# Rounded high and low parts for the heads' projections and three gate tiles; gathered rows in quarter rows turned by VectorE

## The reference

```python
h = modulate(rmsnorm(x, norm_mix), shift1, scale1)
proj = h @ w_in                      # q, k, v, o (4 heads x 256 each), gates, u, ga, gb
q, k, v, o, gates, u, ga, gb = split(proj, IN_SPLITS)
# mLSTM: per head chunkwise scan of q, k, v with gates from the columns `gates`, times sigmoid(o)
# S5: complex-diagonal scan of u, gelu(z) * sigmoid(z @ w_glu + b_glu)
merged = sigmoid(ga) * (h_a @ w_pA) + sigmoid(gb) * (h_b @ w_pB)
x = x + gate1 * (merged @ w_out)
h = modulate(rmsnorm(x, norm_ffn), shift2, scale2)
# expert choice: each of 16 experts takes its top 64 latent and top 16 context tokens
aff = softmax(h @ w_router + b_router); topv, topi = top_k(aff.T, cap)
xe = h[topi]
hid = silu(xe @ w1) * (xe @ w3)      # 1024 -> 1536
x = x + gate2 * scatter_add((hid @ w2) * topv)
y = rmsnorm(x, norm_final)
```

## Time and profile before

| what | value |
|---|---|
| median of 3 runs | 1770.94 us (1770.35 to 1771.46) |
| the profiled execution | 1768.68 us, span 1766.9 us |
| mean granted TensorE clock | 0.971 |
| TensorE (matmul) busy | 1646.3 us, 93% |
| VectorE busy | 602.6 us, 34% |
| ACT busy | 355.5 us, 20% |
| POOL busy | 61.1 us, 3% |
| moved by DMA | 418.68 MB, mean 237 GB/s |

### The profile page before, as it was taken

The page is one execution under the profiler, slowest core; times in us unless marked ns, Lnnn a source line. Parts: engine busy times, 40 slices in busy tenths (PEclk is TensorE's granted clock), DMA queues, the critical chain, the costliest instruction groups (busy, mean ns, idle before and its releaser), DMA issues. The chain is left out here.

```text
span 1766.9 us, 33347 instructions
## 1 busy us (share of the span) xinstructions
PE 1646.3 (93%) x15118; PEld 934.8 (53%) x15118; DVE 602.6 (34%) x1351; ACT 355.5 (20%) x731; POOL 61.1 (3%) x76
## 2 busy tenths in 40 slices
PE   5999999999999999798975999999999999999992
PEld 2566665546464564598963344444444444444441
DVE  6878961013112131477645011111111111111113
ACT  5243332122212223355333000000000000000001
POOL 0000000000000000000001000000000000000000
PEclk9999999999999999999998999999999999999996
DMA  9345463101102021143307899999999999999974
GB/s 391 121 145 178 154 224 141 48 0 70 50 0 107 12 84 56 41 173 125 144 36 302 317 401 397 407 407 406 408 409 407 407 407 408 414 411 410 417 310 134
DMA packets 56913, 418.68 MB, mean 237 GB/s; under 512 B 10932, under 2 KB 17716, under 8 KB 27076
## 3 DMA queue, kind: packets, MB, share of 16 engines
q1 hardware_dynamic: 49188, 385.09, 54.6%
q0 software_dynamic: 6864, 28.85, 5.3%
q10 hardware_dynamic: 720, 2.62, 0.4%
HBM read 389.98 MB, written 24.42 MB: 235 GB/s over the span
## 5 line engine op out<-in xcount | busy, mean ns | idle before, releaser
L1780 PE MATMUL bank<-place,x 128*32 128x384 f32 x3120 | 258.1, 489 | 0.9 <-ACT x L1831 0.9
L1780 PE MATMUL bank<-ring_tail,x 128*32 128x384 f32 x3024 | 248.2, 486 | 0.0
L1780 PEld LDWEIGHTS bank<-place,x 128*32 128x32 f32 x3120 | 100.4, 110 | 147.3 <-issue 143.9
L1780 PEld LDWEIGHTS bank<-ring_tail,x 128*32 128x32 f32 x3024 | 97.8, 110 | 142.9 <-issue 141.6
L1870 DVE TENSOR_TENSOR xT<-sq,bank 128x384 f32<-128x384 f32 x48 | 23.7, 549 | 435.8 <-issue 362.3
L1856 DVE SCALAR_TENSOR_TENSOR hT<-bank,gvr,xT 32x256 f32<-32x256 f32 (+1 forms) x192 | 92.1, 480 | 201.0 <-PE bank L1802 198.4
L1099 PE MATMUL bank<-place,hT 128*128 128x512 f32 x320 | 138.0, 592 | 0.0
L244 PE MATMUL bank<-hT,xT 128*128 128x512 f32 x256 | 131.9, 597 | 1.1 <-ACT qk L254 0.9
L1802 PE MATMUL bank<-place,xT 128*32 128x256 f32 x2304 | 126.7, 379 | 0.0
L1802 PE MATMUL bank<-ring_tail,xT 128*32 128x256 f32 x2304 | 126.5, 379 | 0.0
L1831 ACT ACTIVATE x<-bank 128x320 f32<-128x320 f32 x32 | 12.2, 434 | 542.1 <-PE bank L1765 542.1
(11 more groups left out here) (353 smaller groups left out, 1827.8 us busy)
## 6 DMA issues: line engine op xcount, KB each, us to landing
place<-w_e_dram SPq DMA_DIRECT2D x97, 1536.0 KB, 17.8
ring_tail<-w_e_dram SPq DMA_DIRECT2D x95, 1536.0 KB, 17.2
place<-w_ada_dram SPq DMA_DIRECT2D x12, 2048.0 KB, 9.9
xT<-w_gate_dram POOLq DMA_DIRECT2D x8, 1024.0 KB, 6.4
place<-w_qk_dram SPq DMA_DIRECT2D x4, 2048.0 KB, 11.3
place<-w_vo_dram SPq DMA_DIRECT2D x4, 2048.0 KB, 10.8
place<-w_pAB_dram SPq DMA_DIRECT2D x4, 1536.0 KB, 7.7
hT<-gates_dram SPq DMA_DIRECT2D x4, 1280.0 KB, 5.9
```

What stands on the lines that cost most here:

```text
L1780: mm = pe.matmul(PS[bank + j][TJ * g:TJ * g + TJ, 0:FC], x[:, e % 2, 2 * c + k, TJ * j:TJ * j + TJ], w[:, k, FC * g:FC * g + FC], start=(c ...
```

## The change

Three parts.

**Projections.** `hT` is split once into `h_high` (fp32r, in the region of `xT`, by ACT) and `h_low` (in place of `hT`, by VectorE). The weights of a head are taken in four chunks of 256 columns (`chunk_end`, `chunk_of`); each chunk is rounded by ACT (`round_weights`) into one of two buffers in what was the third slot of the ring, and its remainder is written over the raw weights by VectorE (`split_weights`). `project_features` (q, k and gate tiles) and `project_tokens` (v and o) make three products each, into three banks instead of two. The gate tiles 13 to 15 come as one more piece, `w_gtail`, in two chunks. The GLU comes ahead of the first projection instead of between its units. The ring has two slots for the heads, and the slots and the order of loads for the merge block change.

**Gather.** The routing block also computes, per expert and quarter row, an index 4 x token + quarter (`topq`, `gidx4`). `gather` becomes three indirect DMAs of 128 quarter rows (1 KB) each. VectorE turns them with one transpose of 32 x 32 blocks (`turn_x`), and the rows of w_e1 and w_e3 are put in that order by the host. TensorE's transposes, ACT's `take_x` and POOL's memset go.

**Queues.** SP, ACT, VectorE and TensorE take these steps in the order of the diff, cut to its core:

```diff
+        NU = 16
+        NU_S5 = 13
+        NCH = 4 * H + 2
+        UNITS = 18
+        def chunk_end(c):
+            return UNITS * (c // 4) + ((4, 8, 13, 18)[c % 4] if c < 4 * H else (4, 6)[c - 4 * H])
+        for h in range(H):
+            plan.append((ar["w_qk"][h], "units_done", chunk_end(4 * h + 1), 0))
+            plan.append((ar["w_vo"][h], "units_done", chunk_end(4 * h + 3), 1))
+        plan.append((ar["w_gtail"], "units_done", chunk_end(NCH - 1), 0))
+        def chunk_of(memory, c):
+            if c < 4 * H:
+                x, n, at = memory[:, 2 * (c % 4 // 2):2 * (c % 4 // 2) + 2], 512, 256 * (c % 2)
+            else:
+                x, n, at = memory[:, 0:2], 384, 256 * (c % 2)
+            return x.rearrange("p x n -> p (x n)")[:, 0:KD * n].rearrange("p (k n) -> p k n", k=KD)[:, :, at:min(at + 256, n)]
+        def chunk_raw(c):
+            return chunk_of(place, c)
+        def chunk_low(c):
+            return chunk_of(place_r, c)
+        def chunk_high(c):
+            n = 256 if c + 1 < NCH else P
+            return place_r[:, 4 + c % 2, 0:KD * n].rearrange("p (k n) -> p k n", k=KD)
...
+        MERGE_SLOTS = (1, 2, 0, 2, 0, 1)
...
-                load_weights(sp, CH_H + NSLOT)
+                load_weights(sp, CH_H + 2)
                 for h in range(H):
                     if h:
+                        load_weights(sp, CH_H + 2 * h + 3)
...
+                def project_features(c, u):
+                    pe.wait_ge(sem("w_low_ready"), c + 1)
+                    high, low = chunk_high(c), chunk_low(c)
+                    for m in range(high.shape[2] // P):
+                        for x in range(2):
+                            bank_free(u)
+                            t = slice(x * TH, (x + 1) * TH)
+                            n = slice(m * P, (m + 1) * P)
+                            for k in range(KD):
+                                pe.matmul(PS[u % 3][:, 0:TH], high[:, k, n], h_high[:, k, t], start=(k == 0), stop=False)
+                                pe.matmul(PS[u % 3][:, 0:TH], high[:, k, n], h_low[:, k, t], start=False, stop=False)
+                                mm = pe.matmul(PS[u % 3][:, 0:TH], low[:, k, n], h_high[:, k, t], start=False,
+                                               stop=(k == 7))
+                            mm.then_inc(sem("units_done"), 1)
+                            u += 1
+                def project_tokens(c, u):
+                    pe.wait_ge(sem("w_low_ready"), c + 1)
+                    high, low = chunk_high(c), chunk_low(c)
+                    for t in range(NT):
+                        bank_free(u)
+                        tt = slice(t * P, (t + 1) * P)
+                        for k in range(KD):
+                            pe.matmul(PS[u % 3][:, 0:DH], h_high[:, k, tt], high[:, k, :], start=(k == 0), stop=False)
+                            pe.matmul(PS[u % 3][:, 0:DH], h_high[:, k, tt], low[:, k, :], start=False, stop=False)
+                            mm = pe.matmul(PS[u % 3][:, 0:DH], h_low[:, k, tt], high[:, k, :], start=False,
+                                           stop=(k == 7))
+                        mm.then_inc(sem("units_done"), 1)
+                        u += 1
                 def proj_qk(h):
...
+                for m in range(4):
+                    glu(m)
+                pe.wait_ge(sem("h_low_ready"), KD)
                 proj_qk(0)
...
+                def round_weights(c):
+                    if c < NCH:
+                        have_weights(act, chunk_piece(c))
+                        if c >= 2:
+                            act.wait_ge(sem("units_done"), chunk_end(c - 2))
+                        act.activation(chunk_high(c), chunk_raw(c), ACT.Copy).then_inc(sem("w_high_ready"), 1)
...
+                    for j in range(8):
+                        m, t = j // 2, slice(j % 2 * TH, (j % 2 + 1) * TH)
+                        u = UNITS * h + j
+                        act.wait_ge(sem("units_done"), u + 1)
+                        act.activation(qk[:, h % 2, m, t], PS[u % 3][:, 0:TH], ACT.Copy,
                                        scale=DH ** -0.5 if m < 2 else 1.0).then_inc(sem("proj_copied"), 1)
-                    act.wait_ge(sem("qk_done"), 5 * h + 5)
-                    for x in range(2):
-                        ins = act.activation(qk[:, h % 2, 2 * x:2 * x + 2, LAT:TOK],
-                                             PS[2][:, 256 * x:256 * x + 256].rearrange("p (m t) -> p m t", m=2),
-                                             ACT.Copy, scale=1.0 if x else DH ** -0.5)
-                    ins.then_inc(sem("proj_copied"), 1)
+                        if j % 4 == 0:
+                            round_weights(4 * h + j // 4 + 1)
...
+                    for j in range(2 * NT):
+                        u = UNITS * h + 8 + j
+                        act.wait_ge(sem("units_done"), u + 1)
+                        if j < NT:
+                            act.activation(vt[:, h % 2, j, 0:DH], PS[u % 3][:, 0:DH],
+                                           ACT.Copy).then_inc(sem("proj_copied"), 1)
+                        else:
+                            act.activation(og[:, h % 2, j - NT, :], PS[u % 3][:, 0:DH],
+                                           ACT.Sigmoid).then_inc(sem("proj_copied"), 1)
+                        if j % NT == 0:
+                            round_weights(4 * h + j // NT + 3)
...
+                act.wait_ge(sem("gate_out0"), 16 * 7)
+                act.wait_ge(sem("gate_out1"), 16 * 6)
+                for k in range(KD):
+                    act.activation(h_high[:, k, :], hT[:, k, :], ACT.Copy).then_inc(sem("h_high_ready"), 1)
+                round_weights(0)
                 act.wait_ge(sem("z_in"), 8)
                 for m in range(4):
                     act.activation(hbT[:, m, :], zT[:, m, :], ACT.Gelu_apprx_tanh).then_inc(sem("gelu"), 1)
+                for m in range(4):
+                    glu_sigmoid(m)
...
+                def split_weights(c):
+                    dve.wait_ge(sem("w_high_ready"), c + 1)
+                    dve.tensor_tensor(chunk_low(c), chunk_raw(c), chunk_high(c).bitcast(F32),
+                                      ALU.subtract).then_inc(sem("w_low_ready"), 1)
...
+                    if h + 1 < H:
+                        split_weights(4 * h + 7)
+                        split_weights(4 * h + 8)
...
+                for k in range(KD):
+                    dve.wait_ge(sem("h_high_ready"), k + 1)
+                    dve.tensor_tensor(h_low[:, k, :], hT[:, k, :], h_high[:, k, :].bitcast(F32),
+                                      ALU.subtract).then_inc(sem("h_low_ready"), 1)
+                split_weights(0)
...
+                for c in range(1, 5):
+                    split_weights(c)
                 for h in range(H):
                     weigh(h)
+                    for c in range(4 * h + 5, min(4 * h + 7, NCH)):
+                        split_weights(c)
                     combine(h)
...
-                    load_weights(sp, CH_M + m + 2)
                     sp.wait_ge(sem("branch_used"), 8 * (m - 1))
                     load_sigmoids(m)
+                    load_weights(sp, CH_M + m + 2)
...
+                v(dve.tensor_scalar(topf[:, CAPL:CAP], topf[:, CAPL:CAP], float(LAT), None, ALU.add))
+                for j in range(NJ):
+                    n = min(TJ, CAP - TJ * j)
+                    for g in range(NG):
+                        ins = dve.tensor_scalar(topq[:, j, g, 0:n], topf[:, TJ * j:TJ * j + n], 4.0, float(g),
+                                                ALU.mult, ALU.add)
+                ins.then_inc(sem("route_step"), 1)
...
-                    pool.indirect_dma_start(out=xe[:, e % 2, :], out_offset=None, in_=ar["h2"][:, :],
-                                            in_offset=bass.IndirectOffsetOnAxis(ap=gidx[:, e:e + 1], axis=0)
-                                            ).then_inc(sem(f"xe_in{e % 2}"), 16)
+                    for j in range(NJ):
+                        pool.indirect_dma_start(out=xe[:, e % 2, j, :], out_offset=None, in_=h2q,
+                                                in_offset=bass.IndirectOffsetOnAxis(ap=gidx4[:, j, e:e + 1], axis=0)
+                                                ).then_inc(sem(f"xe_in{e % 2}"), 16)
...
-                        if name == "w1" and c == 1 and e + 1 < E:
-                            turn_x(e + 1)
...
+                def turn_x(e):
+                    dve.wait_ge(sem(f"xe_in{e % 2}"), 16 * NJ * (e // 2 + 1))
+                    if e >= 2:
+                        dve.wait_ge(sem("piece_used"), piece_at["w3", e - 2, 3] + 1)
+                    dve.transpose(x[:, e % 2].rearrange("p j k c -> p (j k c)"),
+                                  xe[:, e % 2].rearrange("p j d -> p (j d)")).then_inc(sem("x_turned"), 1)
+                turn_x(0)
                 dve.wait_ge(sem("gate2_ready"), 1)
                 for e in range(E):
```

(2 more changed lines are left out.)

## The result

The changed kernel takes 1712.65 us (median of 4 runs, 1711.69 to 1713.13) where the kernel before takes 1771.2 (4 runs beside it, 1770.35 to 1772.22): a ratio of 0.967, 95% interval 0.965 to 0.969, 58.5 us less. The forecast was 1717, with 1704 to 1740 as its range. The profiled execution took 1712.79 us, with a span of 1710.9 against 1766.9: 56.0 less. (The profiled execution before lay 2.5 us under its median, so the pair of traces shows that much less than the runs.)

What follows compares the result with a forecast made beforehand. The prediction took TensorE to bound the heads, with DMA as busy as TensorE in the expert stage. Its terms, -47.7 + 1.7 - 7.0 + 4.2 - 5.0 = -53.8 us, gave 1714.9 profiled and a median of 1717, range 1704 to 1740.

Steps and rivals of the forecast that it cites:

- The projections: Head projections on TensorE: 57.0 us per head in place of 68.9, -47.7 us over four heads.
- Rival (c): Head projections: a 256-column product costs as much as one of 320, +26 us, 1743; chance 6%.
- (e): Head projections: weight loads are not hidden behind one-pass products, +256 us, near 2027; chance 2%.
- Preparation at nothing: Rounding and splitting of weight chunks on ACT and VectorE: ready at 8.9 us, over five us spare, costed at nothing.
- Rival (d): Weight chunks in the heads: preparation comes late, 1.5 us at each of 16 chunks, +24 us, 1741; chance 5%.
- Gate tiles: Two gate-tile stretches of 18.5 and 9.7 us become 144 products, 21.2 us: -7.0 us.
- Start of the block: GLU moved ahead of the first projection must wait for VectorE's copies of the turned blocks: +1.7 us, bounds 0 and +6.
- Routing and first gather: From top-k to first expert: extra routing operations +2.4, first gather as three indirect DMAs +1.8, together +4.2 us.
- Expert stage: TensorE loses the turns (12.0 us), but gathers 0.4 us dearer let DMA set the pace late: -5.0 us.
- Rival (a): Expert stage: TensorE keeps the pace, -12.0 us in place of -5.0, 1710; chance 14%.
- Rival (b): Expert stage: gathers cost the lagging DMA engines 1.5 us more each, +14 us, 1731; chance 12%.
- the queue change in the merge stage is costed at nothing: Merge-stage weight loads: the changed queue leaves every piece at least eight steps (14 us), so no cost.

Runs made afterwards that it cites:

- prep_2: Changed kernel with ACT rounding and VectorE going over each weight chunk twice, from the second chunk on; 1710.14 us, ratio 0.966 to the kernel before.
- prep_3: Changed kernel with ACT rounding and VectorE going over each weight chunk three times, from the second chunk on; 1750.13 us, ratio 0.988 to the kernel before.

## Why the prediction was right, point by point

**The projections** (-47.7 forecast, -48.7 measured) were right by their mechanism and to 1 us: TensorE sets the time, 0.147 us holds for 320 columns, and 0.120, worked out for 256, is 0.119. Rival (c) is refuted by it, and so is (e), whose 2027 left out the -6 of the other terms (2021). The windows above have TensorE's loads busy as long as its products, 0.188 us each under products of 0.119: they are hidden, all rows in use. By the rule cited from the Trainium skill (TensorE: Matmul & The Clock Gate, The mechanism) they would not be; here the trace disagrees, as the earlier trace rows had said.

**Preparation at nothing**: right. Ready 8.4 us into the chunk (8.9 forecast), and the two runs with more passes show both the cover and its end. Rival (d) is refuted.

**Gate tiles** (-7.0): exact. **Start of the block** (+1.7 forecast, +2.9 measured): the wait for VectorE is there and comes to 2.1 us (5.8 us from the turning of z to the GLU, for 3.7 to the first projection). The other 0.8 is the clock, which the forecast left out: it is at half from 279 to 289, and costs the GLU 2.2 us where it cost the first projection 1.4 before.

**Routing and first gather** (+4.2 forecast, -0.1 measured): two parts, of which the second failed. The routing costs about what was said, +2.4 (twelve operations 1.08 us, another memset; from the same step of the top-k to the first issue 13.1 us for 11.1, +2.0). The gather was mis-sized, +1.8 forecast and -2.2 measured: the three issues of 1.0 us and the gaps of 0.3 came as forecast, but VectorE has the rows 3.1 us behind the end of the third issue, where TensorE had them 6.8 us behind the end of the one, and one VectorE transpose of 0.98 us stands in the place of TensorE, ACT and their handovers.

**Expert stage** (-5.0 forecast, -12.4 measured): the step that failed is the price of the gather, "I take +0.4, near the 1 KB row", with "The lower end is 0". Measured it is -0.6 us per expert. The forecast priced the gather's own packets alone and put what they do to the weights beside them at nothing, without a reason. For the packets themselves it was wrong in form and near in size: they move as 96 packets of 4 KB and not as 384 of 1 KB, and cost +0.1 us. But the weights beside the old gather were slowed, 535 to 539 ns per packet for 469, and the new gather took that away. (304 more packets per expert would be 4864 more on q0. There are 624: 256 of 4 KB and 496 of 4 bytes more, and 128 fewer of one load of gate weights. That load and the larger gathers are 1 MB each, so that q0 moves 28.85 MB before and after by chance.) The weights' DMA needed 734.0 us from the first expert to the last landing (743.9 before), and TensorE 746.0. Rival (a) is what happened: 46.50 us to the end, landings of 26.7 us. "So what looks like 12.0 us is mostly taken back" is wrong: it is kept whole. Rival (b) is refuted. The best guess on the rings that GpSimd's DMAs keep (the Trainium skill, DMA: Bandwidth & Descriptors, Latency and other measured facts) would have made more indirect DMAs dearer on the late engines; no run shows such a price.

**What the forecast left out** took back what the last two terms gave, so that the total still came out near 1717. The drain behind the new gather costs +2.6 (the end has +2.3 in all); it takes 5.27 us in the traces of seven kernels with that gather, the change among them, and 2.65 in the three with the old one. The barrier behind the heads costs +3.2: "the queue change in the merge stage is costed at nothing" asked only whether the weights are late, not what they run beside. And the scores at a lower clock cost +3.1. That is no accident of one execution: in ten of the twelve traces with the changed heads the scores of the second and of the third head take 13.0 us, and in the two with the old heads 11.43 to 11.47 (`prep_2` has 10.28 at one of the places, `prep_3` 11.38 at both). Over the heads' block the granted clock is at half for 20.5 us in both traces with the old heads, and for 30.7 to 34.1 us in nine of those with the new. The five terms of the sum came to -65.2 in place of -53.8, and what had stood at nothing to +9.2 (the 1.7 us ahead of the block are among them).

So the time lies near the forecast for a mixed reason, in part by luck: the heads came by their mechanism, routing and experts brought 11.7 us more than forecast, the experts by rival (a), and three small costs that were left out took most of it back.

**Open**: why the drain takes 2.6 us more (it took 5.06 with twice as many gathers, so it does not go by their number), what lowers the granted clock behind a turn and more so with the changed heads, and which property of the old gather slows the weights beside it.

## What to carry to other kernels

Price a product by its columns and passes from the trace, and then ask of every DMA that a change moves which barrier or store now runs beside it; ends of blocks are on the path even where their engine is idle. Where a transfer changes its form, price also what it does to the transfers beside it: compare their GB/s, or their time per MB, beside it and away from it. Don't let a bound stop at zero without a reason. Before work is taken off an engine that runs level with DMA, measure the floor by leaving some of that work out: here it is 10 us below the stage.

## What the runs showed of the hardware that was not expected

- Three indirect DMAs of 128 rows of 1 KB move as 96 packets of 4 KB. Weight packets of 12 KB beside them take 469 ns; beside one indirect DMA of 80 rows of 4 KB they take 535 to 539, which costs 0.6 us more per gather where DMA sets the pace.
- POOL's drain at a block's end takes 5.27 us with the new gather and 2.65 with the old, though all transfers have landed when it begins.
- Six indirect DMAs per expert in place of three halt TensorE for 2.2 us per expert ("issue"), with no piece of weights late.
- Weight loads with records of 0.188 us are hidden under one-pass products of 0.119 us that use all rows.
- Stalls of the same length, 2.6 us, left the granted clock at 1.00 in one kernel and were followed by 0.61 in another.
